# Mixture-of-experts stage of a two-layer decoder trunk: the gather of token rows in two rounded parts, and the fullest expert moved from last to third

## The reference, cut to what matters

```python
def grouped_moe(h, router_w, router_b, w_gu, w_down):
    ...
    gate_dense = jnp.sum(jax.nn.one_hot(experts, N_EXPERTS, dtype=jnp.float32) * gates[..., None], axis=1)
    gu = jnp.einsum('td,edf->etf', t, w_gu)
    g, u = split_cols(gu, (EXPERT_FF, EXPERT_FF))
    act = jax.nn.silu(g) * u * gate_dense.T[:, :, None].astype(t.dtype)
    y = jnp.einsum('etf,efd->td', act, w_down)
```

## Time and profile before

| what | value |
|---|---|
| median of three executions | 1073.78 us (1069.72 to 1075.07) |
| the profiled execution: time | 1065.87 us |
| the profiled execution: span | 1063.9 us |
| mean granted TensorE clock | 0.926 of full speed |
| busy: TensorE matmul, VectorE, ScalarE | 88%, 39%, 16% |
| expert stage of layer 0 | about 215.7 to 495.5 us |
| expert stage of layer 1 | about 790.4 to 1051.3 us |

### The profile page before, as it was taken

How to read it: one execution, slowest core, us unless ns; L and a number is a source line. 1 busy time by engine, 2 the same in 40 slices (tenths; PEclk the granted TensorE clock), 3 DMA queues, 4 the chain that set the end, 5 groups by cost and what they waited for, 6 DMA issues and landing times.

```text
span 1063.9 us, 13148 instructions
## 1 busy us (share of the span) xinstructions
PE 935.1 (88%) x5454; PEld 609.6 (57%) x5454; DVE 416.1 (39%) x984; ACT 171.2 (16%) x416; POOL 13.0 (1%) x51
## 2 busy tenths in 40 slices
PE   2699789499999899896999989987769999999994
PEld 2385554475556455452868777764356555555551
DVE  4846575442131311311796754543251111111112
ACT  2121120221111011102101422340111111111101
POOL 1000000000000000000000000000000000000000
PEclk9999789689999999898999989957859999999998
DMA  9996644647999999999377331170209799999941
GB/s 353 387 382 238 226 158 158 237 184 295 408 405 409 404 408 408 405 399 378 120 263 286 130 118 54 70 313 1 79 13 407 306 409 408 409 408 409 409 164 41
DMA packets 96079, 294.13 MB, mean 276 GB/s; under 512 B 2448, under 2 KB 3088, under 8 KB 96016
## 3 DMA queue, kind: packets, MB, share of 16 engines
q1 hardware_dynamic: 95184, 289.89, 70.7%
q10 hardware_dynamic: 688, 2.82, 0.7%
q0 software_dynamic: 144, 0.52, 0.1%
HBM read 292.18 MB, written 1.05 MB: 276 GB/s over the span
## 4 chain that ended last, share of the span: by engine, by line
PE 50%; issue 26%; DVE 11%; DMA 6%; SPq 4%; ACT 3%; POOL 0%; DVEq 0%; POOLq 0%
PE bank L618 13%; PE bank L614 9%; PE bank L801 9%; DMA ring<-w_gu_dram 4%; DVE gb L1190 4%; SPq L406 4%; PE bank L816 3%; PE bank L792 3%; PE bank L647 2%; PE bank L669 2%; PE bank L830 2%; PE bank L546 2%; PE bank L566 1%; DMA ring<-ada_w_dram 1%; PE bank L554 1%
## 5 line engine op out<-in xcount | busy, mean ns | idle before, releaser
L801 PE MATMUL bank<-ring,scr 128*64 128x256 f32 x2176 | 253.7, 387 | 9.4 <-DMA ring<-w_gu_dram 9.4
L801 PEld LDWEIGHTS bank<-ring,scr 128*64 128x64 f32 x2176 | 155.0, 139 | 102.2 <-issue 20.8
L618 PE MATMUL bank<-hT,ring 128*128 128x256 f32 x640 | 145.7, 389 | 0.0
L618 PEld LDWEIGHTS bank<-hT,ring 128*128 128x128 f32 x640 | 124.2, 196 | 17.9 <-issue 0.5
L816 PE MATMUL bank<-ring,scr 128*64 128x512 f32 x544 | 122.6, 592 | 0.0
L1190 DVE SCALAR_TENSOR_TENSOR gb<-ring,small,gb 128x512 f32<-128x512 f32 x140 | 105.5, 754 | 5.0
L1640 DVE TENSOR_TENSOR scr<-bank,scr 128x256 f32<-128x256 f32 x34 | 14.4, 424 | 205.3 <-ACT scr L1130 205.3
L792 PEld LDWEIGHTS bank<-scr,xh 128*128 128x128 f32 x576 | 71.6, 203 | 24.5 <-issue 22.0
L792 PE MATMUL bank<-scr,xh 128*128 128x128 f32 x576 | 77.8, 292 | 2.3 <-DVE scr L1612 2.3
L816 PEld LDWEIGHTS bank<-ring,scr 128*64 128x64 f32 x544 | 38.9, 137 | 64.4 <-issue 59.8
L1112 ACT ACTIVATE scr<-bank 128x256 f32<-128x256 f32 (+1 forms) x52 | 23.4, 450 | 300.5 <-PE bank L809 237.7
(11 more groups left out here) (215 smaller groups left out, 684.3 us busy)
## 6 DMA issues: line engine op xcount, KB each, us to landing
ring<-w_gu_dram SPq DMA_DIRECT2D x64, 2048.0 KB, 21.6
ring<-w_down_dram SPq DMA_DIRECT2D x32, 2048.0 KB, 21.4
ring<-ada_w_dram SPq DMA_DIRECT2D x24, 2048.0 KB, 17.6
ring<-od_w_in_dram SPq DMA_DIRECT2D x9, 2048.0 KB, 14.2
ring<-ev_w_in_dram SPq DMA_DIRECT2D x5, 2048.0 KB, 17.4
ring<-ev_w_out_dram SPq DMA_DIRECT2D x2, 2048.0 KB, 9.7
ring<-od_w_out_dram SPq DMA_DIRECT2D x2, 2048.0 KB, 11.0
xs<-x_dram ACTq DMA_DIRECT2D x1, 1024.0 KB, 5.8
```

The lines of the kernel that those rows point to most:

```text
L618: ins = pe.matmul(banks[h][:, m * 256:(m + 1) * 256], w[:, c, (2 * h + m) * P:(2 * h + m + 1) * P], x_part[:, c, :], start=(c == 0 and m = ...
L801: ins = pe.matmul(b[64 * m:64 * m + 64, 256 * u:256 * u + 256], h[:, c, :], w[:, c, 512 * u + 256 * m:512 * u + 256 * m + 256], start=(fir ...
```

## The change

1. **Gather in two parts.** `xh` is split into `x_hi` (a rounded copy, float32r) and `x_lo` (the remainder, float32r), and the gather runs over both, so each of its products is two float32r matmuls where it was one float32 matmul. The maps are float32r too.
2. **Four blocks at a time.** The 17 blocks fall into groups of 2, 2, 4, 4, 4 and 1, with maps 128, 128, 256, 256, 256 and 64 columns wide. Rows of a group of four are gathered in four portions of two chunks; for the group of blocks 4 to 7 two portions each fall in iterations 2 and 3, one of them through bank 3, for the others one portion in each of four iterations.
3. **The fullest expert third.** Blocks 2 and 3 both use position 2, and position k > 2 belongs to block k + 1. D of position 2 is loaded before X of position 3.
4. The sums of the `A` panels move one iteration later, and buffers move to make room (`scr` in two parts, some expert buffers now in `hT`). In `route` the second map is now built before `order` is written.

```diff
 def position(b):
-    return min(b, POS - 1)
+    return b if b <= 2 else b - 1
...
-    for k in range(2, POS):
-        out += [("X", k), ("Y", k)]
-        if k >= 3:
-            out.append(("D", k - 1))
+    out += [("X", 2), ("Y", 2), ("D", 2), ("X", 3), ("Y", 3)]
+    for k in range(4, POS):
+        out += [("X", k), ("Y", k), ("D", k - 1)]
         if ada and k % 4 == 1:
             out.append(("A", k // 4))
     return out + [("D", POS - 1)]
+GROUPS = [(0, 2), (2, 4), (4, 8), (8, 12), (12, 16), (16, 17)]
+FIRST_ROWS = [(0, 0, 2), (0, 1, 3)]
+ROWS_AT = {0: [(1, 0, 2)], 1: [(1, 1, 2)], 2: [(2, 0, 2), (2, 1, 3)], 3: [(2, 2, 2), (2, 3, 3)], 12: [(5, 0, 2)]}
+ROWS_AT.update({4 + n: [(3, n, 2)] for n in range(4)})
+ROWS_AT.update({8 + n: [(4, n, 2)] for n in range(4)})
+SLOTS_AT = {1: 2, 2: 3, 5: 4, 9: 5}
...
-        if l == 0 and b % 4 == 2:
+        if l == 0 and b % 4 == 3:
             out.append(("A", b // 4))
...
+        x_hi, x_lo = sb("x_hi", [P, T, D], F32R), sb("x_lo", [P, T, D], F32R)
+        slots = sb("slots", [P, 2, T, 4 * SLOTS], F32R)
...
-            def gather(b, half, slots, width):
-                for c in range(4):
-                    cc = 4 * half + c
+            def gather(b, ccs, slots, w):
+                for c, cc in enumerate(ccs):
                     for t in range(T):
-                        ins = pe.matmul(b[:, c * width:(c + 1) * width], xh[:, t, cc * P:(cc + 1) * P],
-                                        slots[:, t, 0:width], start=(t == 0), stop=(t == T - 1))
+                        for x_part in (x_hi, x_lo):
+                            ins = pe.matmul(b[:, c * w:(c + 1) * w], x_part[:, t, cc * P:(cc + 1) * P],
+                                            slots[:, t, 0:w], start=(t == 0 and x_part is x_hi),
+                                            stop=(t == T - 1 and x_part is x_lo))
...
-                    if b != POS - 1:
+                    if b != 2:
                         ins.then_inc(panel_done[pl.slot], 1)
                     elif half == 1:
                         ins.then_inc(first_done, 1)
...
-                half_rows(0, 0)
-                half_rows(0, 1)
+                pe.wait_ge(lo_ready, 2 * (l + 1))
+                for g, n, k in FIRST_ROWS:
+                    rows(g, n, k)
...
-                    if 2 * j < BLOCKS:
-                        half_rows(j, b % 2)
+                    for g, n, k in ROWS_AT.get(b, []):
+                        rows(g, n, k)
...
+                if s == 1:
+                    for t in range(T):
+                        act.activation(x_hi[:, t, :], xh[:, t, :], ACT.Copy).then_inc(hi_ready, 1)
...
+                if s == 1:
+                    for t in range(T):
+                        dve.wait_ge(hi_ready, 2 * l + t + 1)
+                        dve.tensor_tensor(x_lo[:, t, :], xh[:, t, :], x_hi[:, t, :].bitcast(F32), ALU.subtract)\
+                           .then_inc(lo_ready, 1)
...
-                step(dve.tensor_copy(rgs[:, :, 15], sel6))
-                dve.tensor_copy(order[:, 2:16], rgs[:, 5, 2:16]).then_inc(order_ready, 1)
+                dve.tensor_copy(rgs[:, :, 2], sel6)
+                dve.tensor_copy(rgs[:, 2:4, 3], sel6[:, 2:4])
+                step(dve.tensor_scalar(rgs[:, 0:2, 3], sel6[:, 0:2], -float(SLOTS), None, ALU.add))
                 slot_map(pcur[1], rgs, 1)
...
+                dve.tensor_copy(order[:, 2:3], rgs[:, 5, 2:3])
+                dve.tensor_copy(order[:, 3:16], rgs[:, 5, 4:17]).then_inc(order_ready, 1)
```

More of the change, by code:

```diff
@@ L79, in body_items, with group_of, width, chunks @@
     return out + [("D", POS - 1)]
+GROUPS = [(0, 2), (2, 4), (4, 8), (8, 12), (12, 16), (16, 17)]
[4 more added lines that the diff above has]
+SLOTS_AT = {1: 2, 2: 3, 5: 4, 9: 5}
+def group_of(b):
+    return next(g for g, (a, z) in enumerate(GROUPS) if a <= b < z)
+def width(g):
+    return SLOTS * (GROUPS[g][1] - GROUPS[g][0])
+def chunks(g, n):
+    per = 512 // width(g)
+    return range(n * per, (n + 1) * per)
 def y_uses():
-    out = [("H0", 0)]
+    out = [("H", g, n) for g, n, k in FIRST_ROWS if k == 2]
     for b in range(BLOCKS):
-        j = b // 2 + 1
-        if 2 * j < BLOCKS:
-            out.append((f"H{b % 2}", j))
+        out += [("H", g, n) for g, n, k in ROWS_AT.get(b, []) if k == 2]
         if b:
@@ L94, in t_uses @@
 def t_uses(l):
-    out = [("H1", 0)]
+    out = [("H", g, n) for g, n, k in FIRST_ROWS if k == 3]
     for b in range(BLOCKS):
@@ L100, in t_uses @@
             out.append(("T", b - 1))
+        out += [("H", g, n) for g, n, k in ROWS_AT.get(b, []) if k == 3]
         if b % 2 == 1 or b == BLOCKS - 1:
             out.append(("PT", b // 2))
-        if l == 0 and b % 4 == 2:
+        if l == 0 and b % 4 == 3:
             out.append(("A", b // 4))
@@ L214, in trunk @@
         flag = sb("flag", [P, 2], I32)
-        SCR = 12416
-        scr = sb("scr", [P, SCR])
+        HEAD, TAIL = 7168, 5632
+        scr = sb("scr", [P, HEAD])
+        mod = sb("mod", [P, 2, 48])
+        table = sb("table", [P, 344])
+        order = sb("order", [P, 16], I32)
+        rb_row = sb("rb_row", [P, 16])
+        with nc.sbuf_tensor("tail", [P, TAIL], F32) as tail:
+            pass
         bank = [ctx.enter_context(nc.psum_tensor(f"bank{b}", [P, 512], F32)) for b in range(8)]
@@ L226, in view @@
                 n *= d
+            if base is scr and off >= HEAD:
+                base, off = tail, off - HEAD
             v = base[:, off:off + n]
@@ L1602, in route, with slot_map @@
                 dve.tensor_scalar(flag[:, l:l + 1], cmax[:, 0:1], 0.0, None, ALU.is_gt).then_inc(flag_ready, 1)
-            def columns(j):
-                return [c for c in (2 * j, 2 * j + 1) if c < BLOCKS]
-            def slot_map(dst, table, j):
-                for k, c in enumerate(columns(j)):
+            def slot_map(dst, table, g):
+                for k, c in enumerate(range(*GROUPS[g])):
                     for t in range(T):
@@ L1616, in slot_gates @@
             def slot_gates(dst, table, j):
-                for k, c in enumerate(columns(j)):
+                for k, c in enumerate(range(2 * j, min(2 * j + 2, BLOCKS))):
                     for t in range(T):
@@ L1652, in ada_end, with rows @@
                     ada_add(1, a, bank[3]).then_inc(t_free, 1)
-                dve.wait_ge(t_full, t_at(l, "H1", 0))
-                gather_cols(hg[0], l, 1, bank[3], P).then_inc(t_free, 1)
+                def rows(g, n, k):
+                    dve.wait_ge(*((h_full, h_at(l, "H", g, n)) if k == 2 else (t_full, t_at(l, "H", g, n))))
+                    rows_in_place(hg[g % 2], l, chunks(g, n), bank[k], width(g)).then_inc(y_free if k == 2 else t_free, 1)
+                rows(0, 1, 3)
                 for b in range(BLOCKS):
-                    j = b // 2 + 1
                     if b >= 1:
```

168 lines of the change are left out of this document (81 added, 87 removed).

## The result

Seven executions of the changed kernel, in turn with seven of the kernel before on the same chip, gave a median of 1064.43 us (1058.08 to 1066.62) against 1070.13 us. The ratio is 0.993, with a 95% interval from 0.990 to 0.996: faster by some 6 us, where 15.5 us less were forecast (1058 us, counted from a median of 1073.78). The direction and the range held, and so did much of the mechanism; more than half of the gain is missing.

A forecast was written before the change was run, and what follows sets the result against it. TensorE and the DMA were taken to run almost level in the expert stages. Layer 0's 7 us and layer 1's 8.7 made about 15.5 us less: 1050.4 us profiled, 1058 against the median; range 1048 to 1077.

The forecast's parts named there:

- One record by the weight load, 0.124 us at all widths: In the gather, loading weights paces each float32r matmul, 0.124 us at any width, so a group costs 4.0 us.
- Rival 4: In the gather, float32r is as dear as float32 at all widths: 57 us more, 1131 us; chance 0.06.
- rival 2: In the gather, the weight load is cheaper and records go by columns, 0.053 us at 128: 1051 us; chance 0.12.
- The first group at 5.0 us: At each expert stage's start, the first gather group at the lower clock takes 5.0 us, like the router's 32 records.
- Rival 1: Groups 0 and 1: float32r at 128 columns no faster than float32 by column, 15 us lost, 1073 us; chance 0.24.
- Layer 1 ended by the DMA at 1042.6: Layer 1's end: D15 lands at 1036, 6.4 us of work follow, so the stage ends 8.7 us earlier.
- TensorE's own end: Layer 1: TensorE alone would end at 1039.1 us, the gather saving 13.5 us and bank 3 costing 1.3.
- Layer 0 was forecast at 7 us less: Layer 0's stage ends at 487.5 to 488.5 us, 7 to 8 us less, with 7 taken; block 15's wait stays.
- Bank 3: Iteration 3: the transposed gate map waits for VectorE to empty bank 3, 1.3 us once per layer.
- The split: Copies to x_hi on ScalarE and subtractions on VectorE, before the gather: covered by TensorE's router matmuls, costing nothing.
- Route: The second map before order makes order about 1 us later in route; no panel is delayed, cost nothing.
- The ring: Y5 waits for D2's slot, free at 289.4 us in layer 0; 30 panels at 5.13 to 5.25 us follow.

The follow-up runs named there:

- the repeat: The changed kernel run again with nothing altered, measured against the kernel before: 1064.46 us, ratio 0.995.
- A0 early: The changed kernel with the sum of panel A0 one iteration earlier, so that Y4 starts earlier: 1062.88 us, ratio 0.994 to the kernel before.
- the order alone: The changed kernel's groups of four and new order, but the gather in float32: 1067.89 us, ratio 0.998; with the fullest at position 8, 1059.81 us, 0.990.

## Why the prediction came out half right

**One record by the weight load, 0.124 us at all widths: right.** It is 0.11 us at 64 and 128 columns and 0.12 at 256. Rival 4 (float32r as dear as float32, 0.455 us) is out, and so is rival 2, which wanted 0.053 us at 128 columns (at 256, where it wanted 0.114, the two can't be told apart). The Trainium skill (TensorE: Matmul & The Clock Gate, LDWEIGHTS) has a weight load take, in ns, the number of weight columns over 1.2, by which I estimate 107 ns for 128; the 0.11 us agree with it, at the full clock. At the lower clock they are 0.21.

**The first group at 5.0 us, and nothing said of what stands behind it: this step failed.** I sized it, "at the lower clock", by the router's 32 records of 5.04 us. That row was not at the lower level: the granted clock over it was 0.71, since it rose on the way. In the execution after it stayed at the lower level, and the same 32 records took 6.98 us. The busy time over the router before (columns of the earlier trace rows), and the router after:

```profile
773.79:778.80 5.01, 5.01 (x32) 4.93 (x32) 0.00 (x0) 0.00 (x0) 0.00 (x0) 0.71 0.00 0
```

```profile
772.99 6.98 PE L809 MATMUL bank<-col,hT 128*128 128x16 f32 x32 [1.22 <-issue]
```

And I took for granted that the clock would rise in the first group as it did before. The group took 7.0 us in both layers, 2.0 more, and the `up` behind it lost another 2.6 us in layer 0 (6.24 for 3.67) and 1.3 us in layer 1 (4.94). The sum has it nowhere. It stands before Y5's issue. So in layer 0 Y5 left at 294 us in place of 289.4, X14 landed at 452.6 in place of 448, and the stage ended at 492.5 in place of 487.5 to 488.5: one shift of 4.5 us carried through. Rival 1 had this place and the way a shift carries, but the wrong price: it looked for dear records, and at the full clock the narrow records are cheap; it is the lower clock in and behind them that is dear. What gives it back is float32 in the narrow groups: 4 us with the fullest third, 7 us in the stages with the fullest at position 8 (9.6 between the medians).

**Layer 1 ended by the DMA at 1042.6: the panels came later, and the path was the wrong one.** Put against this execution, whose first gather starts 1.2 us later, Y5 should have left at 865.2 us, D15 have landed at 1037.2 and the stage have ended at 1043.8. The issues of Y5 and of D14 and D15 (the latter at 1017.1 us), and KB and time to landing of these two:

```profile
867.75 0.37 SPq L440 DMA_DIRECT2D ring<-w_gu_dram  x1
...
1012.13 11.10 SPq L440 DMA_DIRECT2D ring<-w_down_dram  x2
```

```profile
ring<-w_down_dram SPq DMA_DIRECT2D x2, 2048.0 KB, 24.9
```

D15 landed at 1042.0 us, 4.8 us late: 2.5 of them for Y5 (the slow `up` and bank 3, with nothing saved in the first group to cancel them), the rest because the 33 panels took 174.3 us from Y5's issue in place of 171 to 172. But D15 was not the panel that counted. TensorE's last wait for weights is 0.78 us for X15, at 1026.80 us, and from there it works without another to the end, 23.1 us later. I had counted the 6.4 us behind D15 and not the 23.1 us behind X15, which lands 15.2 us before it; that path is some 1.5 us the longer. In the three other profiles with a late X15 (the repeat, A0 early, narrow groups in float32) it is 23.1 us too. Later panels and longer path are the 6 us by which the stage ended late.

TensorE's own end I had put at 1040.3 by this count, and without its one wait it would have come at 1049.1, so it was 8.8 us off and almost level with the loads again. The gather's busy time there, before and after:

```profile
790.00:1052.00 262.00, 39.42 (x288) 36.29 (x288) 0.99 0.85 339
```

```profile
790.00:1050.00 260.00, 29.61 (x192) 27.00 (x192) 0.97 0.87 342
```

It saved 9.8 us in place of 13.5: 2.0 in the first group, some 0.7 in the slow records at 975 us (0.1 each), the rest at the ends of the portions. To these 3.7 us come the first `up` (1.3) and the one at 976.87 us (6.21 for 3.67, 2.5): 7.5 of the 8.8 us. Of the fall at 975 us, 3.2 us in all, I had no step either. Since TensorE was already waiting for the loads, by 0.8 us, giving it its time back in the narrow groups moved this stage by 1.7 us and no more; the whole 4.8 us showed only at position 8.

**What was luck.** The time, 1064.43 us, is 9.4 us under the 1073.78 that I counted from, but 3.7 of these are only that those three executions lay above the median of seven. Layer 0 was forecast at 7 us less and gave 2.9, layer 1 at 8.7 and gave 2.6. With the narrow groups in float32, that is without the step that failed, layer 0 gives 6.4 us, close to the forecast, and layer 1 still only 4.3.

**Bank 3: right,** 1.18 us for 1.3 in each layer. **The split: right, nothing.** The router's matmuls cover it, and `route` starts at 203.89 us, before at 204.18. The rows of the split and of the first step behind it:

```profile
198.28 2.01 ACT L1034 ACTIVATE x_hi<-xh 128x1024 fp32r<-128x1024 f32 x2
...
199.38 2.36 DVE L1294 TENSOR_TENSOR x_lo<-xh,x_hi 128x1024 fp32r<-128x1024 f32 x2 [2.64 <-ACT x_hi L1034]
...
203.89 0.19 DVE L1575 TENSOR_REDUCE small<-bank 128x2 f32<-128x32 f32 x1 [2.15 <-PE bank L809]
```

**Route: right,** `order` comes at 220.16 us, half a microsecond later (I had 1), and no panel is late by it.

**The ring: right.** The hold ends with D2's slot, as counted; the experiment on A0 rules out the other slot. The DMA moved its 30 panels from 294 to 452.6 us, 5.3 us each, just above the 5.13 to 5.25 I gave. The 39.5 us from X14 to the end were 39.9.

**What to look for:** of the signs that I named for being right, the 0.12 us, the waits at blocks 11 and 15 and the dry DMA came. The first group of 5 us did not, nor D15 near 1036 us less what layer 0 gave, and of the short waits in layer 1 only one came, at block 16. The first of these was the one that mattered.

## What to carry to other kernels

When a group of matmuls is replaced by cheaper ones, price the instructions behind it too: the group's own time can fall while the granted clock of what follows drops, and then a place where TensorE is busy without a gap is slower than before, as the first `up` here (6.24 us for 3.67). Where two engines run level, what a change is worth hangs on what else has been relieved: the two-part gather in the wide groups gave 7 us with the fullest third and 14 at position 8. But compare like with like, with the narrow groups the same on both sides, and don't write off a part for one bad place: the order alone gave 0.2% with the fullest third and 1.0% at position 8. Look for every panel that is waited for near the end, and count the work behind each, not behind the last alone. Here work that reuses loaded data did best where the ring had just run empty, neither before, where its hold stopped loads, nor after, where the waits had begun; count for each load which slot it takes and what frees it.

## What the runs showed of the chip that I had not expected

- A float32r matmul with 128 x 128 weights is one instruction, 0.11 us after the one before at 64 and 128 columns and 0.12 us at 256. The float32 one is two, and at the full clock these stand 0.11 us apart as well at 64 and 128 columns (0.124 is the mean over a portion of 16 with its end) and 0.22 us at 256. So two float32r parts cost the same as one float32 matmul at 128 columns, and little more than half of it at 256.
- The granted clock stayed low (0.50) through a first group of float32r records of 128 columns and came back only within the next 32 matmuls, in 12 of 12 stages; behind float32 records in the same place it was at the full level, in 16 of 16.
- It fell while TensorE was busy without a gap, within the 64-column float32r records, to 0.52 over the next 5 us (975 to 980 us), and stayed there for the next `up`: in layer 1 in six profiles of six, in layer 0 within the group in one and right behind it in two. With the same group in float32 it fell there in none of 14 stages, in seven profiles.
- At the lower clock the float32r records are 0.21 us apart, at 64 columns as at 128, and the float32 ones at 128 too: what paces them is not the columns, and it slows with the clock.
